# Joining two chunks of a delta-rule inverse in TensorE's hand-written program, and moving the small matmuls around it

## What is computed

```python
g = jnp.cumsum(g, axis=-1)
decay = chunk_decay(g)                       # exp(g_i - g_j) for i >= j, else 0
k_beta = k * beta[..., None]
a_mat = jnp.einsum("bnhid,bnhjd->bnhij", k_beta, k) * decay * strict
t_mat = lax.linalg.triangular_solve(eye + a_mat, eye, left_side=True, lower=True, unit_diagonal=True)
u = jnp.einsum("bnhij,bnhje->bnhie", t_mat, v * beta[..., None])
w = jnp.einsum("bnhij,bnhjd->bnhid", t_mat, k_beta * jnp.exp(g)[..., None])
def step(S, inp):
    v_new = u_c - jnp.einsum("bhcd,bhde->bhce", w_c, S)
    o = jnp.einsum("bhcd,bhde->bhce", qd_c, S) + jnp.einsum("bhij,bhje->bhie", qk_c, v_new)
    S = S * jnp.exp(gl_c)[..., None, None] + jnp.einsum("bhcd,bhce->bhde", kd_c, v_new)
    return S, o
```

## Time and profile before

| | us |
|---|---|
| median of 3 executions | 2826.65 |
| the profiled execution | 2822.21 |
| its span, first to last instruction | 2820.4 |
| TensorE busy in the span | 2514.7 (89%) |
| GpSimd | 1666.4 (59%) |
| VectorE | 1486.1 (53%) |
| ScalarE | 1170.1 (41%) |
| TensorE's mean granted clock | 0.95 |

### The profile page before, as it was taken

One profiled execution on the slowest core, in us unless ns is written; L12 is line 12 of the kernel. 1 busy time (PEld: TensorE's weight loads), 2 busy tenths in 40 slices (PEclk: granted clock), 3 DMA queues, 4 the chain that ended last, 5 costly groups with the idle time before them and its releaser, 6 DMA issues.

```text
span 2820.4 us, 57876 instructions
## 1 busy us (share of the span) xinstructions
PE 2514.7 (89%) x20918; PEld 2295.1 (81%) x20918; DVE 1486.1 (53%) x3373; ACT 1170.1 (41%) x2073; POOL 1666.4 (59%) x2236
## 2 busy tenths in 40 slices
PE   6988898988988889898999988888898889799997
PEld 5877777877877778787999888877887779699987
DVE  5555555555556555555132426676767776722242
ACT  4433343433343344434333444444454435433343
POOL 4544444434444454434887667666766677598765
PEclk8999999999999999999999999999999999899999
DMA  4333333323333333322644336545654466354433
GB/s 183 115 128 120 135 120 135 107 105 109 129 120 128 127 135 120 127 95 103 215 154 153 115 124 237 180 134 174 228 189 147 162 214 201 108 213 150 153 119 116
DMA packets 126773, 410.86 MB, mean 146 GB/s; under 512 B 21344, under 2 KB 37984, under 8 KB 122112
## 3 DMA queue, kind: packets, MB, share of 16 engines
q1 hardware_dynamic: 81216, 295.75, 30.0%
q10 hardware_dynamic: 45504, 114.38, 11.7%
HBM read 363.47 MB, written 46.61 MB: 145 GB/s over the span
## 4 chain that ended last, share of the span: by engine, by line
issue 34%; POOL 31%; PE 22%; DVE 10%; ACT 2%; DMA 1%; POOLq 0%; ACTq 0%; DVEq 0%
POOL wl L324 31%; PE psj L347 6%; PE psj L349 6%; PE psj L348 6%; DVE arena L1368 5%; DVE arena L1366 2%; ACT arena L1205 1%; DVE arena L1706 1%; DVE arena L1697 1%; PE psA L736 1%; PE psE L354 1%; DVE arena L1704 1%; PE psE L691 0%; PE psA L354 0%; DMA arena<-s_rows_d 0%
## 5 line engine op out<-in xcount | busy, mean ns | idle before, releaser
L324 POOL TENSOR_TENSOR wl<-ring,wh 128x256 fp32r<-128x256 f32 x2232 | 1666.2, 785 | 1131.4 <-ACT wh L787 1130.3
L347 PE MATMUL psj<-xh,wh 128*128 128x288 f32 x4400 | 1390.5, 316 | 105.3 <-DVE arena L1474 59.6
L348 PE MATMUL psj<-xl,wh 128*128 128x288 f32 x4400 | 1316.2, 299 | 0.0
L349 PE MATMUL psj<-xh,wl 128*128 128x288 f32 x4400 | 1311.4, 298 | 0.0
L347 PEld LDWEIGHTS psj<-xh,wh 128*128 128x128 f32 x4400 | 841.4, 191 | 182.1 <-issue 80.9
L348 PEld LDWEIGHTS psj<-xl,wh 128*128 128x128 f32 x4400 | 845.2, 192 | 6.5 <-issue 3.9
L349 PEld LDWEIGHTS psj<-xh,wl 128*128 128x128 f32 x4400 | 845.3, 192 | 0.0
L787 ACT ACTIVATE wh<-ring 128x1024 fp32r<-128x1024 f32 x558 | 564.9, 1056 | 245.1 <-PE psj L349 217.3
L1368 DVE SCALAR_TENSOR_TENSOR arena<-arena 128x256 f32<-128x256 f32 (+1 forms) x672 | 287.9, 494 | 2.6
L855 ACT ACTIVATE arena<-psj 128x256 f32<-128x256 f32 x112 | 43.1, 385 | 472.6 <-PE psj L349 462.0
L407 PE MATMUL psD<-h 128*32 128x256 f32 x512 | 75.1, 460 | 32.8 <-DMA h<-gstate_d 32.8
(11 more groups left out here) (311 smaller groups left out, 2999.2 us busy)
## 6 DMA issues: line engine op xcount, KB each, us to landing
ring<-weights_d SPq DMA_DIRECT2D x558, 512.0 KB, 3.3
h<-gstate_d ACTq DMA_DIRECT2D x16, 1024.0 KB, 8.7
gst_s_d<-h ACTq DMA_DIRECT2D x16, 1024.0 KB, 3.9
h<-sstate_d ACTq DMA_DIRECT2D x32, 512.0 KB, 6.3
sst_s_d<-h ACTq DMA_DIRECT2D x32, 512.0 KB, 5.0
arena<-g_rows_d ACTq DMA_DIRECT2D x16, 864.0 KB, 4.6
arena<-s_rows_d ACTq DMA_DIRECT2D x8, 1152.0 KB, 7.6
h_spill_d<-h ACTq DMA_DIRECT2D x2, 2304.0 KB, 7.8
```

Source lines behind the costliest of these rows:

```text
L324: ins = pool.tensor_tensor(wl[:, s, n:n + 2], ring[:, s, n:n + 2], wh[:, s, n:n + 2].bitcast(F32), ALU.subtract)
L347: pe.matmul(out, w_h, xh[:, kt, :], start=(kt == 0), stop=False)
L348: pe.matmul(out, w_h, xl[:, kt, :], start=False, stop=False)
L349: mm = pe.matmul(out, w_l, xh[:, kt, :], start=False, stop=(kt == KT - 1))
```

## The change

What it does:

- **Inverse.** Chunks 0 and 1 are handled as four units at once. Slot 7+2l has P of all four, slot 8+2l has Q of all four (first the products for D, then those for E, with a semaphore each: g_qd, g_qe). VectorE has one mask (256 columns a partition) in place of two of 128, then one subtraction for D (g_dd) and one for E (g_de). P of the next level waits only for g_dd. The tap stands between mask and subtraction as before; B (g_bs) stands at level 1, is awaited at slot 12, and the other sample copy at level 4.
- **Sample readout and mask transposes** go from slot 3 to slot 18, behind the last products; they write bank D, and ScalarE copies them behind the values of v.
- **Transposes of v** go from slot 19 to 17. New values, the products and the updates that follow stand one slot earlier (20, 22, 23, 25, 26, 27, 29, 30). The output's transposes go from 36 to 37, the norm sums from 39 to 40.
- **Decay rows.** ScalarE loads the next head's rows right behind the sample copy at slot 6 (it waits for g_rf, VectorE's QD) and the pack of v behind the conv output; at the end of the iteration, behind the copies of tile 6's weights and ahead of the load of states, it makes the next head's decays (`g_decays`). VectorE copies the columns for them at the end of the iteration (`columns`, behind the first state update) and keeps the decay factors of the states in a small buffer of their own (gEG, two copies).
- **Beta.** VectorE multiplies beta into the decays before it needs k k^T. The sample masks are made behind QD.

```diff
-                if e == 10:
+                if e == 12:
                     pe.wait_ge(S("g_bs"), m + 1)
-                if e == 27:
+                if e == 26:
                     pe.wait_ge(S("g_sample_act"), m * 4 + SMP_ACT["vnds"])
...
+                def inv_p(lv):
+
+                    if lv == 0:
+                        pe.wait_ge(S("g_d"), m + 1)
+                        pe.wait_ge(S("g_sample_act"), m * 4 + SMP_ACT["asc"])
+                    else:
+                        pe.wait_ge(S("g_dd"), m * 5 + lv)
+                    for u in range(4):
+                        mm = halves(psC, slice(u * 64, (u + 1) * 64), gAT[:, u, :], half(gDE[:, 0], lv, 0)[:, u])
+                    mm.then_inc(S("g_p"), 1)
+
+                def inv_q(lv):
+
+
+                    pe.wait_ge(S("g_pm"), m * 6 + lv + 1)
+                    if lv < 5:
+                        for u in range(4):
+                            mm = halves(psA, slice(u * 64, (u + 1) * 64), gDE[:, 1, u, :], half(gP[:, :], lv, 0)[:, u])
+                        mm.then_inc(S("g_qd"), 1)
+                    for u in range(4):
+                        mm = halves(psE, slice(u * 64, (u + 1) * 64), gP[:, u, :], half(gDE[:, 1], lv, 1)[:, u])
+                    mm.then_inc(S("g_qe"), 1)
+
+                for lv in range(6):
+                    if e == 7 + 2 * lv:
+                        inv_p(lv)
+                    if e == 8 + 2 * lv:
+                        inv_q(lv)
...
+                if e == 18:
                     pe.wait_ge(S("g_mk"), m + 1)
+                    pe.wait_ge(S("g_es"), m + 1)
+                    pe.wait_ge(S("g_st_in"), m * 16 + 16)
                     for r in range(2):
-                        mm = pe.transpose(psF[:, r * P:(r + 1) * P], gMK[:, 4 * r:4 * r + 4, :], ident)
-                    mm.then_inc(S("g_sample_pe"), 1)
-                    pe.wait_ge(S("g_st_in"), m * 16 + 16)
+                        pe.transpose(psD[:, 256 + r * P:256 + (r + 1) * P], gMK[:, 4 * r:4 * r + 4, :], ident)
                     for b in range(DEC_B):
...
-                if e == 36:
+                if e == 37:
                     pe.wait_ge(S("g_on"), m + 1)
...
-                if e == 39 and more:
+                if e == 40 and more:
                     pe.wait_ge(S("g_su"), m * 4 + 2)
                     gdn_norm(m + 1)
...
+            def g_decays(m):
+
+                act.wait_ge(S("g_dtx"), m + 1)
+                act.wait_ge(S("g_r_in"), m * 16 + 16)
...
+                if full:
+                    act.wait_ge(S("g_rf"), m + 1)
+                    g_load_rows(m + 1)
...
+                if full:
+                    g_decays(m + 1)
                 act.wait_ge(S("g_y"), m + 2)
                 act.wait_ge(S("g_st_out"), m * 16 + 16)
                 act.wait_ge(S("g_sp_out"), m * 16 + 16)
                 act.wait_ge(S("g_cv_out"), m * 16 + 16)
                 if full:
-                    g_load(m + 1)
+                    g_load_states(m + 1)
...
+                def mask_p(lv):
+                    dve.wait_ge(S("g_p"), m * 6 + lv + 1)
+                    dve.tensor_tensor(half(gP[:, :], lv, 0), packed(psC[:, 0:2 * P], lv),
+                                      half(bc(cst[:, K_LEV + lv, :], 1, 4), lv, 0), ALU.mult) \
+                        .then_inc(S("g_pm"), 1)
+
+                def less_q(lv):
+
+
                     if lv < 5:
+                        dve.wait_ge(S("g_qd"), m * 5 + lv + 1)
+                        D = half(gDE[:, 0], lv, 0)
+                        dve.tensor_tensor(D, D, packed(psA[:, 0:2 * P], lv), ALU.subtract).then_inc(S("g_dd"), 1)
+                    dve.wait_ge(S("g_qe"), m * 6 + lv + 1)
```

More of the change, by code:

```diff
@@ L398, in gdn_mix @@
                         .then_inc(S("g_tok"), 1)
-                if e == 3:
+                if e == 5:
+                    pe.wait_ge(S("g_e1"), m + 1)
+                    for c in range(NC):
+                        for j in range(2):
+                            mm = pe.transpose(psB[:, (2 * c + j) * P:(2 * c + j + 1) * P], gDE[:, 1, 2 * c + j, :],
+                                              ident)
+                    mm.then_inc(S("g_dt"), 1)
+                if e == 6:
+                    for j in range(2):
+                        mm = pe.transpose(psE[0:NS, 64 + NS * j:64 + NS * (j + 1)], gATS[:, j, :], ident[0:NS, 0:NS])
+                    mm.then_inc(S("g_sample_pe"), 1)
@@ new lines, in gdn_mix @@
+                for lv in range(6):
[3 more added lines that the diff above has]
+                        inv_q(lv)
+                if e == 7:
+                    for j in range(2):
+                        mm = pe.matmul(psD[0:NS, 256 + NS * j:256 + NS * (j + 1)], gATS[:, j, :], gAS[:, j, :],
+                                       start=True, stop=True)
+                    mm.then_inc(S("g_sample_pe"), 1)
+                if e == 12:
+                    for j in range(2):
+                        mm = pe.matmul(psD[0:NS, 320 + NS * j:320 + NS * (j + 1)], gBS[:, j, :], gNS[:, j, :],
+                                       start=True, stop=True)
+                    mm.then_inc(S("g_sample_pe"), 1)
@@ L421, in inv_p @@
-                def inv_p(c, lv):
-                    if lv == 0:
-                        pe.wait_ge(S("g_d"), m + 1)
-                        pe.wait_ge(S("g_sample_act"), m * 4 + SMP_ACT["asc"])
-                    else:
-                        pe.wait_ge(S(f"g_de{c}"), m * 6 + lv)
-                    for j in range(2):
-                        mm = halves((psC, psE)[c], slice(j * 64, (j + 1) * 64), gAT[:, 2 * c + j, :],
-                                    half(gDE[:, c, 0], lv, 0)[:, j])
-                    mm.then_inc(S(f"g_p{c}"), 1)
@@ L433, in inv_q @@
-                def inv_q(c, lv):
-                    pe.wait_ge(S(f"g_pm{c}"), m * 6 + lv + 1)
-                    if lv == 0:
-                        pe.wait_ge(S("g_sample_act"), m * 4 + SMP_ACT["kmc"])
-                    bank = (psA, psF)[c]
-                    if lv < 5:
-                        for j in range(2):
-                            halves(bank, slice(j * 64, (j + 1) * 64), gDE[:, c, 1, j, :],
-                                   half(gP[:, 2 * c:2 * c + 2], lv, 0)[:, j])
-                    for j in range(2):
-                        mm = halves(bank, slice((2 + j) * 64, (3 + j) * 64), gP[:, 2 * c + j, :],
-                                    half(gDE[:, c, 1], lv, 1)[:, j])
-                    mm.then_inc(S(f"g_q{c}"), 1)
@@ L1533, in gdn_body @@
                 states(0)
+                if full:
+                    columns(m + 1)
                 dve.wait_ge(S("g_rs2"), m + 1)
@@ L1572, in _ @@
             dve.wait_ge(S("g_ccolc"), 1)
+            columns(0)
             dve.wait_ge(took_act, 6)
```

207 lines of the change are left out of this document (85 added, 122 removed).

## The result

The changed kernel takes 2843.84 us, the kernel before 2819.86 us (medians of 12 runs each). The ratio is 1.0083, its 95% interval 1.0064 to 1.0102: **slower by 0.8%**, where I had forecast 2750 us and given "slower" a chance of 0.04. Sign and range were both wrong. One of the twelve runs fell in the chip's slower state (3106.9 us, clock 0.76), and the ratio leaves it out.

The account below looks back on a forecast made before the run. It took TensorE's own program, its waits (8.2 us) and clock loss (3.1) to bound the 79.0 us iteration. Floor 67.1 + waits 5.95 + clock 1.1 = 74.2, 4.8 less, 77 us over sixteen iterations: 2750 us, range 2695 to 2790.

Parts of the forecast that it names:

- Removed waits and the floor: GDN iteration: slot 10's 3.73 us and slot 3's 2.8 vanish; without waits and clock loss it takes 67.1 us.
- Slots 5 and 6: VectorE's front chain delivers E in time for TensorE but N late, a wait of +0.8 us in slot 6.
- Slot 3 goes: Moving the sample readout to slot 18 removes slot 3's two waits, 2.8 us; the readout costs the same there.
- The rule I cited: VectorE-GpSimd SBUF lock, held for a whole instruction; by it every instruction of the first tap would be held too.
- Slots 9 and 11: Value-convolution taps delay the inverse's P: +0.2 us for the first tap, +1.0 in slot 11 for the second.
- Slots 25 and 26: TensorE arrives earlier and waits for ScalarE's scaled copy behind tile 2, +1.5 us.
- Slot 37: TensorE's wait for the normalised output before its transposes, 2.05 us instead of 1.70.
- Slot 0: Its projection waits for GpSimd's first half of low weights, +0.4 us.
- The clock, +1.1: Loss to the lowered TensorE clock per iteration falls from 3.1 to 1.1 us, all given to slot 37.
- The clock does not recover: Rival: six waits replace four and the clock falls as often; 2.0 us an iteration, 2782 us; chance 0.15.
- GpSimd holds the first tap as well: Rival: the first tap's four instructions lose 1.6 us too; +0.8 us an iteration, 2763 us; chance 0.12.
- Slower: Rival: in the joined inverse TensorE waits 0.63 us for VectorE's mask in each of twelve halves; +45, 2872 us; chance 0.04.

Follow-up runs that it names:

- e10: e5 with the output's transposes behind slot 38 and VectorE's loop-end wait moved as in e2; 2665.63 us, ratio 0.9458.
- e8: The change with each GpSimd subtraction covering a quarter of its columns, leaving three quarters of the low weights out of the result; 2618.30 us, ratio 0.9297.
- e2: The change with VectorE's wait for ScalarE's copy of tile 7 moved from the loop's end to just ahead of the inverse; 2813.23 us, ratio 0.9974.
- e5: The change with the readout back in slot 3, masks at the end of VectorE's iteration, and the later block in its old slots; 2695.15 us, ratio 0.9586.
- e6: The change with only the block behind slot 18 back in its old slots, readout still at 18; 2776.11 us, ratio 0.9854.
- e1: The change with 16 dummy matmuls ahead of slot 5's wait for E and 8 ahead of slot 6's for N; 2798.48 us, ratio 0.9915.
- e9: The change with readout in slot 3, masks at VectorE's iteration end, and 13 dummy matmuls ahead of slot 37's wait; 2722.09 us, 2756.99 without the dummies.
- e4: The kernel before with the joined inverse alone; 2738.88 us, ratio 0.9714.

## Why the prediction was wrong

**Removed waits and the floor: right.** Slot 10's 3.73 and slot 3's 2.8 went, and the readout at 18 has no wait before it. My floor without waits and clock loss was 67.1 us. e10, whose waits are 1.5 us an iteration, takes 68.8: 67.3 without them. Only its starting point was read too coarsely: with 3.5 us lost to the clock in the kernel before, the floor would be 66.7. What the floor left out is where the forecast failed.

**Slots 5 and 6, "E is in time and N is not", +0.8: wrong, and with the clock behind it (below) the step that turned the sign.** Measured are 2.34 + 1.23 = 3.6 us. TensorE's arrival and the decays were right: the norm sums of the iteration stand at 477.25, slot 0 comes 7.9 behind (7.8 forecast), the decays 8.3 (8.4). Then I had E at 13.0; it came at 492.75 - 477.25 = 15.5. Of these 2.5 us, 0.9 is the loop-end wait for L848, with the turn of the loop behind it: it was in the program, and I had followed what ScalarE's decays did to its own later copies ("needed eight slots on: nothing") without asking who waits for the tile copy behind them. The rest is the length of the chain, 6.3 us instead of 4.6. I took the durations from the earlier trace rows, where GpSimd was done at 488.66, ahead of E (kernel before, same iteration, GpSimd):

```profile
477.87 10.79 POOL L324 TENSOR_TENSOR wl<-ring,wh 128x256 fp32r<-128x256 f32 x14
```

The change starts the chain 1.3 us behind slot 0 instead of 6.0, and all of it lies in a burst of 13.61 us. I had the contention in view for the taps, and did not apply it to the chain that I moved. e8 shows it by itself: with a quarter of GpSimd's columns the chain takes 4.3 us.

**"Slot 3 goes", -2.8: right.** That TensorE comes earlier without the readout was counted as well; what it was held against, the chain, was 2.5 us too short.

**The rule I cited.** The row at 500.90 shows the first tap's four operations taking 2.87 us beside a burst that began at 500.13, where the same took 1.39; the second tap took 1.20:

```profile
500.90 2.87 DVE L1377 TENSOR_SCALAR arena<-arena 128x256 f32<-128x256 f32 x4
...
505.64 1.20 DVE L1379 SCALAR_TENSOR_TENSOR arena<-arena 128x256 f32<-128x256 f32 x4
```

The Trainium skill, page "SBUF — State Buffer", section "Who interferes with whom", has VectorE operations with two SBUF inputs and those in a two-port mode (copies and tensor_scalar can enter one) contend with GpSimd, and those with at most one SBUF input outside these modes not. The Trainium skill says only of the two-port modes that the lock is held for the whole instruction. By that rule the first tap is held as well, and so is the front chain, and the trace agrees on both, down to L1433, which reads PSUM and took 0.69. The product with beta (L1429), with two SBUF inputs, took 0.67 in the change, in e2 and in e5 alike, and that it does not explain; L1426 took 0.68 in the change and 1.23 in e2. I had the rule as a rival at +13 us for the tap alone. The place that mattered was the chain.

**Slots 9 and 11, +1.2: 0.6 measured.** GpSimd's burst hangs on slot 7's end, as forecast, and so does the inverse's first product. But that product ran at the lower clock (1.12 us at 498.53), and the first tap's four operations came behind the burst's start; the second tap's began at 505.64, when the burst was nearly over (505.82). In e10, at full clock, both taps are held, and P waits 14.5 us in 31 times, 0.9 an iteration:

```profile
512.91 2.41 DVE L1378 TENSOR_SCALAR arena<-arena 128x256 f32<-128x256 f32 x4
...
517.00 2.35 DVE L1380 SCALAR_TENSOR_TENSOR arena<-arena 128x256 f32<-128x256 f32 x4
```

**Slots 25 and 26, +1.5: right** (1.2 measured). **Slot 37, 2.05: right** (2.03). **Slot 0, +0.4**: in the loop some 0.3.

**The clock, +1.1: wrong, and the largest error.** 6.4 us were lost. I had argued that "none is as long as slot 10's was" and given nothing to slots 5 and 6. But two waits of 2.0 and 1.4 us, close together, brought the clock down in all fifteen iterations (0.52 in the windows), and slot 37's in 13 of 15, where slot 36's had done so in 3 before the change and in 8 in e6. e1 and e9 show it: with the same data arriving at the same time they are 45 and 35 us faster.

**The rivals.** "The clock does not recover" was the right mechanism with the wrong size: I had bounded it by the loss before, 3.1 us (3.5 by the clock records), as though a change could only give back what was lost, and could not lose more. "GpSimd holds the first tap as well" was right in its mechanism (2.87 and 2.41 us for 1.39), but it moved the time little. "Slower" I had placed in the round trip of the inverse, which stays closed: levels at full clock take 3.7 us, and e4 alone gains 2.9%. That "slower" was on the list at 0.04 is no credit, since it came by another way.

The balance per iteration, in us:

| | before | forecast | measured |
|---|---|---|---|
| waits | 8.3 | 5.95 | 7.7 |
| lost to the clock | 3.5 (read as 3.1) | 1.1 | 6.4 |
| the rest | 67.0 (read as 67.7) | 67.1 | 66.5 |
| sum | 78.8 | 74.2 | 80.6 |

## What to carry to other kernels

When a block of work is moved away from in front of a wait, look at what runs on the other engines in that time; work that looks like a cost of its own may be the only cover of a chain. When a chain is moved in time, take its durations again from the place where it will stand: the same operation was 0.69 us there and 1.09 here. And a wait on TensorE should be costed with the clock behind it, from rows of both levels: where waits cannot be avoided, dummy matmuls in front of them gave back 45 and 35 us.

## What the runs showed that I had not expected

- A very short VectorE operation can lose the largest factor beside GpSimd: copying 128x2 took 0.72 us in the burst and 0.16 beside the shortened one, a 32x64 product 0.51 for 0.20. Which operation is hit depends on where it falls: in e2 the same copy took 0.15 (472.56) and the product behind it 1.23, in the change 0.72 and 0.68. The chain as a whole took 6.3 to 6.6 us beside the burst in the change, e2 and e5.
- A wait's length does not set its price in clock. The same wait of 1.70 us in slot 36 was followed by a fall of the clock in 0 of 15 iterations in e4, 3 before, 8 in e6 and 9 in e5; the same 2.03 in slot 37 in 6 of 15 in e2, 10 in e1, 13 in e3 and in the change. What else decides it these runs do not show. With the wait filled or covered there was no fall behind it at all (e9, e10).
- An earlier matmul is not an earlier result. The later block's matmuls moved by a slot or two, and their inputs did not: the only effects were waits and clock, 3.6 us an iteration.
